# The low part of a second early weight: from VectorE to GpSimd, and its high part earlier on ScalarE

## The chip, the cores and the metric

The kernel runs on one core of a Trainium2 chip. The metric is the device time of one execution in microseconds (us); the time of a kernel is the median of its runs.

## The reference

Two blocks, one behind the other, over 256 tokens of width 1024 in float32. The first has an even and an odd layer (pooling, retention, memory attention, sparse attention). The second has two layers, each of them with this shape:

```python
h = rmsnorm_2(x, norm_mix[i])
proj = h @ w_in[i]                 # na_q, na_k, na_v, latents, gate_a, gate_b
merged = sigmoid(gate_a) * y_a + sigmoid(gate_b) * y_b
x = x + merged @ w_out[i]
x = x + expert_choice_moe(rmsnorm_2(x, norm_moe[i]), ...)
ple_gate = sigmoid(rmsnorm_2(x, norm_ple[i]) @ ple_gate_w[i])
x = x + ple_gate * (p[i] @ ple_w[i])
```

The change lies at the seam between layer 0 and layer 1 of the second block: the last two lines for `i = 0`, and the first two for `i = 1`.

## The kernel before, in words

The five engines run programs of their own, written out by hand, which meet at semaphores. Weights come from HBM through a ring of 12 slots in SBUF (8 KB a partition each), filled in order by SyncE; TensorE counts the units it has begun (`begun`), and SyncE waits for that count before it fills a slot again.

**Split weights.** A projection is computed from a high and a low part of both operands, with three products (high by high, high by low, low by high). A split weight of 1024 x 256 takes two slots. It lands in the first; ScalarE copies it, rounded, into the second (`split` in its program, L1762: the high part), and then VectorE subtracts the high part from the slot of the first, in place (L2160: the low part). GpSimd has a `split` of its own (L2644), with the same subtraction, used for the weights in `HEADS`: gate weights 0 and 3. VectorE's low parts count up the semaphore `lo_ready`, GpSimd's `heads_low`. Where a unit of TensorE is `late`, it waits for the high part alone before its first products and for the low part (`U.low`) in `tile_rest`.

**The seam.** The tokens are two tiles of 128. In `embed_gates`, TensorE multiplies tile 0 and then tile 1 by the four gate weights (`pg` 0 to 3, 256 columns each; L1335 with the high parts of the weights, L1344 with the low parts). Two weights fill a PSUM bank of 512 columns, so there are four evacuations, called gate 0 and gate 1 (tile 0), gate 2 and gate 3 (tile 1). For each, ScalarE makes a tanh (L1878), and VectorE two scalar_tensor_tensor instructions (L2248, which adds 1 and multiplies by the embedding, both operands in SBUF; L2250, which adds the product to x, both in SBUF too). With gate 1 done, tile 0 of x is final: ScalarE sums its squares (L1748), GpSimd makes the root (L2611, L2612), ScalarE scales the rows (L1752), and TensorE transposes them (L956). These transposes stand in TensorE's queue ahead of the last gate product. The transposed tile is split into high and low parts in `tile_high` (ScalarE, L1791) and `tile_parts` (VectorE, L2119 and eight L2124, one operand in PSUM). Tile 1 goes the same way behind gate 3, with its sum of squares (L2100) and its scale (L2105) on VectorE.

Layer 1 opens in `values_start`: tile 0 by the first two weights of `w_in` that are used, `("nav", 0)` and `("nav", 1)`, then the transposes of tile 1 and tile 1 by the same two. These two weights are called `EARLY`, since they are split at the end of layer 0:

```python
HEADS = [("pg", 0), ("pg", 3)]
EARLY = [("nav", 0), ("nav", 1)]
```

Before the change, both parts of nav 0 are made behind gate 0, and both parts of nav 1 ahead of gate 3, behind `tile_high` on ScalarE and `tile_parts` on VectorE. `split_at` numbers the splits that VectorE counts in `lo_ready`. Behind the seam ScalarE issues the small loads of the next layer (behind gate 3), and GpSimd makes eight bias tiles of the neighbourhood attention when they have landed (L2713); VectorE adds the first in L2446.

Of the kernel before, what the change touches and what calls it, by code (L numbers as in the profile page):

```python
# [23 lines left out]
ALU = mybir.AluOpType  # L24
# [26 lines left out]
LAYERS = 2  # L51
# [242 lines left out]
SPLIT_FIRST = [u for u in FIRST_UNITS if u[0] in SPLIT]  # L294

HEADS = [("pg", 0), ("pg", 3)]
EARLY = [("nav", 0), ("nav", 1)]
SPLIT_LAYER = [u for u in LAYER_UNITS + PLE_UNITS if u[0] in SPLIT and u not in HEADS]
# [102 lines left out]
def build(nc, a, out, at):  # L401

    ctx = ExitStack()
    with ctx:
        def sem(name):
            return ctx.enter_context(nc.semaphore(name))
# [177 lines left out]
        rpb_out, biastile_out = sem("rpb_out"), sem("biastile_out")  # L584
        side_in = sem("side_in")
        lo_ready = sem("weights_low")
        heads_low = sem("heads_low")
        uTh_ready = sem("uT_high")
        spare_in = [sem(f"spare_in{i}") for i in range(SPARES)]
        units_in = [sem(f"unit_in{s}") for s in range(RING)]  # L590
# [71 lines left out]
        def slot_at(l, unit, second=False):  # L662

            if l is None:
                n = FIRST_AT[unit] + second
                return n % RING, n // RING + 1, n - RING + 2 if n >= RING else None
            n = FIRST_SLOTS + LAYER_AT[unit] + second + l * PER_LAYER
            return n % RING, n // RING + 1, n - RING + 2

        def split_at(l, unit):  # L670
            return SPLIT_FIRST.index(unit) if l is None else \
                len(SPLIT_FIRST) + SPLIT_LAYER.index(unit) + l * len(SPLIT_LAYER)

        def words_of(name, *i):

            if name == "out":
                return 2 * D
            i = i[0]
            return KC * {"o_gl": 3 * NH, "lat": LATC}.get(name, 256)

        def rows_of_unit(unit):
            return OUT_ROWS[unit[1]][unit[2]][1] if unit[0] == "out" else P
# [13 lines left out]
        def slot_words(s, n, words=ring):  # L696
            return words[:, s * SLOT:s * SLOT + n]
# [23 lines left out]
        def layer_gains(l):  # L721
            return gT[:, GC_L + l * GL:GC_L + (l + 1) * GL]
# [167 lines left out]
        def _(pe):  # L890
# [3 lines left out]
            class Unit:  # L894
# [3 lines left out]
                def __init__(s, l=None, split=None, double=False, late=False):  # L898
                    s.slot, rnd, _ = w.next()
                    s.low = None  # L900
                    if double:
                        pe.wait_ge(units_in[s.slot], 16 * rnd)
                        pe.sem_inc(units_in[w.next()[0]], 16)
                    elif split:
                        if split in HEADS:
                            s.low = (heads_low, HEADS.index(split) + 1 + l * len(HEADS))
                        else:
                            s.low = (lo_ready, split_at(l, split) + 1)
                        s.high, rnd, _ = w.next()
                        if late:  # L910
                            pe.wait_ge(units_in[s.high], 16 * rnd)
                        else:
                            pe.wait_ge(*s.low)
                    else:
                        pe.wait_ge(units_in[s.slot], 16 * rnd)
                    s.first, s.step = True, Unit.before
                    Unit.before = 2 if split or double else 1
# [34 lines left out]
            unit = [None]  # L952
# [779 lines left out]
        def _(act):  # L1732
# [21 lines left out]
            def split(l, *unit):  # L1754

                s0, rnd, _ = slot_at(l, unit)
                s1, _, free = slot_at(l, unit, True)
                act.wait_ge(units_in[s0], 16 * rnd)
                if free is not None:
                    act.wait_ge(begun, free)  # L1760
                n, r = words_of(*unit), rows_of_unit(unit)
                A(slot_words(s1, n, ring_r)[0:r], slot_words(s0, n)[0:r], ACT.Copy).then_inc(units_in[s1], 16)  # L1762
# [24 lines left out]
            def tile_high(l, j, t, gains):  # L1787

                act.wait_ge(uT_psum, 4 * normT_at(l, j) + 2 * t + 2)
                for k in range(4, KC):  # L1790
                    A(uTh_r[:, k, t * P:(t + 1) * P], banks[5 + 2 * t][:, (k - 4) * P:(k - 3) * P], ACT.Copy,  # L1791
                      scale=gains[:, k:k + 1]).then_inc(uTh_ready, 1)
# [209 lines left out]
            for l in range(LAYERS):  # L2002
# [75 lines left out]
                evacuate(l, "pg", 0)  # L2078
                if l + 1 < LAYERS:
                    split(l + 1, *EARLY[0])  # L2080
                evacuate(l, "pg", 1)
                act.wait_ge(x_ple, TT + 4 * l + 2)
                tile_ss(0, x[:, 0, :])
# [2 lines left out]
                evacuate(l, "pg", 2)  # L2086
                if l + 1 < LAYERS:
                    tile_high(l + 1, 0, 0, layer_gains(l + 1))
                    split(l + 1, *EARLY[1])
                evacuate(l, "pg", 3)  # L2090


# [1 line left out]
        def _(dve):  # L2094
# [59 lines left out]
            def split(l, *unit):  # L2154

                s0, _, _ = slot_at(l, unit)
                s1, rnd, _ = slot_at(l, unit, True)
                dve.wait_ge(units_in[s1], 16 * rnd)
                n, r = words_of(*unit), rows_of_unit(unit)
                V.tensor_tensor(slot_words(s0, n, ring_r)[0:r], slot_words(s0, n)[0:r],  # L2160
                                slot_words(s1, n, ring_r).bitcast(F32)[0:r], ALU.subtract).then_inc(lo_ready, 1)
# [111 lines left out]
            for j, plan in enumerate((EVEN_PLAN, ODD_PLAN_V)):  # L2273
                for entry in plan:
# [67 lines left out]
                    elif what == "RT":  # L2342
                        dve.wait_ge(r_tp, h + 1)
                        c, n = RET_CHUNKS[h][0], len(RET_CHUNKS[h])
# [84 lines left out]
            for l in range(LAYERS):  # L2429
                gl = layer_gains(l)  # L2430
                tile_parts(l, 0, 1, gl)
                for entry in LAYER_PLAN:
                    what, h = entry[0], entry[1]
                    i = att_at(l, h) if what in "STV" else None
# [147 lines left out]
                evacuate(l, "pg", 2)  # L2582
                if more:
                    tile_parts(l + 1, 0, 0, layer_gains(l + 1))
                    split(l + 1, *EARLY[1])
                else:
                    dve.wait_ge(lastg_in, 16)
                    store_rows(0)
# [9 lines left out]
        def _(pool):  # L2598
# [36 lines left out]
                steps.link(g.tensor_tensor(ms[:, c], ms[:, c], neghalf[:, 0:1], ALU.pow))  # L2635
                g.tensor_tensor(rstd[:, c], ms[:, c], lrstd[:, c], ALU.mult).then_inc(norm_rstd[t], 1)

            def split(l, name, i):

                s0, _, _ = slot_at(l, (name, i))  # L2640
                s1, rnd, _ = slot_at(l, (name, i), True)
                pool.wait_ge(units_in[s1], 16 * rnd)
                n = words_of(name, i)
                g.tensor_tensor(slot_words(s0, n, ring_r), slot_words(s0, n), slot_words(s1, n, ring_r).bitcast(F32),  # L2644
                                ALU.subtract).then_inc(heads_low, 1)

            def normalise(h, i, buf):
                pool.wait_ge(recip_done, i + 1)
# [3 lines left out]
            for j, plan in enumerate((EVEN, ODD)):  # L2652
                for entry in plan:
# [14 lines left out]
                    elif entry[1:2] == ("e_za",):  # L2668
                        i = entry[2]
# [37 lines left out]
            for l in range(LAYERS):  # L2707
                if l:
                    norm(l, 0)

                pool.wait_ge(side_in, 64 * (l + 1))
                for h in range(NAH):
                    g.tensor_tensor(  # L2713
                        strided(B_at + h * TT * T, P, (T, TT), (GRIDW, 4), (1, GRIDW)),
                        strided(F_at + h * NBIAS + 2 * NADC, P, (-2 * NADC, TT), (NADC, 4), (1, GRIDW)),
                        con("namask").unsqueeze(1).unsqueeze(1).broadcast_to([P, TT, 4, GRIDW]),
                        ALU.add).then_inc(nabias, 1)
                for entry in LAYER:
                    what, h = entry[0], entry[1]
                    if what == "T":  # L2720
                        normalise(h, att_at(l, h), b_S)
                    if what == "T" and h == NAH - 1:
                        pool.wait_ge(lat_ss, l + 1)
                        for n, wd in enumerate((QR, KVR)):
                            stand(pool)
                            steps.link(g.tensor_scalar(lms[:, 2 * n:2 * n + 2], lss[:, 2 * n:2 * n + 2], 1.0 / wd, EPS,
                                                       ALU.mult, ALU.add))
                        g.tensor_tensor(lrstd, lms, neghalf[:, 0:4], ALU.pow).then_inc(lat_rstd, 1)
                norm(l, 1)
                pool.wait_ge(idx_ready, l + 1)  # L2730
                stand(pool)
                with pool.Fori(0, NE // BATCH) as b:
                    for q in range(BATCH):
                        m = l * NE + b * BATCH + q
                        if q == 0:
                            pool.wait_ge(onehot_ready, l * (NE // BATCH) + b + 1)
                        else:
                            pool.wait_ge(comb_psum, m)
                        g.tensor_tensor(prep, onehot[:, :, q, :].unsqueeze(2).broadcast_to([P, TT, 4, CAP]),  # L2739
                                        affh[:, :, bass.ds(b * BATCH + q, 1)].unsqueeze(3)  # L2740
                                        .broadcast_to([P, TT, 4, CAP]), ALU.mult).then_inc(slots_ready, 1)
                split(l, *HEADS[0])
                for t in range(TT):
                    half_root(l, t)
                split(l, *HEADS[1])
            norm(LAYERS, 0)


# [22 lines left out]
```

## Time and profile before

| | |
|---|---|
| time, median of 3 runs | 1879.73 us (1878.81 to 1879.8) |
| the profiled execution | 1878.34 us, span 1876.6 us |
| TensorE busy, mean granted clock | 1547.2 us (82%), 0.941 of full speed |
| VectorE busy | 634.5 us (34%) |
| ScalarE busy | 517.1 us (28%) |
| GpSimd busy | 197.2 us (11%) |
| HBM | 302 GB/s over the span |

The busy times say how much an engine has to do, not whether anything waits for it. The clock is the one that was granted to TensorE, as a share of 2.4 GHz; 0.50 is the lower level, 1.2 GHz. The profile gives each instruction a start and a duration, and in brackets how long its engine had been idle before it and what ended that. An instruction that is held up while it runs shows as a long one, not as an idle engine.

### The profile page before, as it was taken

Reading aid. Unit: us, or ns where it says so; the run is one execution under the profiler, and the core shown is the slowest. Engines: PE = TensorE matmul, PEld = TensorE weight load, DVE = VectorE, ACT = ScalarE, POOL = GpSimd, SP = SyncE. Lnnn points to the kernel's source line nnn. Section 1 sums busy time; section 2 is a strip of 40 time slices with the busy share of each in tenths; the row PEclk is TensorE's granted clock in tenths of the full one; section 3 lists DMA queues with packets and bytes.
Section 4 is the critical chain, followed back from the end, with each engine's and each line's share of the span. In section 5 each row is a group of like instructions: output and inputs, shape, how many; then the busy total and the mean of one; then the engine's idle time right before and its main releaser. Section 6 shows DMA issues by size and latency. Waiting matters only on the chain.

```text
span 1876.6 us, 29888 instructions
## 1 busy us (share of the span) xinstructions
PE 1547.2 (82%) x12670; PEld 1134.7 (60%) x12670; DVE 634.5 (34%) x934; ACT 517.1 (28%) x921; POOL 197.2 (11%) x215
## 2 busy tenths in 40 slices
PE   9999999999999999656665666999998656766667
PEld 8999899998798885222322323998873322323225
DVE  3556654667556452000000002755540000000005
ACT  3433443456444532000000003454521000000003
POOL 1042000011041100000000002411100000000003
PEclk9999999999999999898888989999999897888879
DMA  9364669423555479999999999644499999999994
GB/s 304 125 208 169 203 231 302 130 97 113 181 152 160 136 314 387 427 425 424 425 427 424 428 425 368 192 145 156 179 381 407 424 426 424 427 426 426 427 425 161
DMA packets 166895, 563.67 MB, mean 300 GB/s; under 512 B 10559, under 2 KB 120027, under 8 KB 133896
## 3 DMA queue, kind: packets, MB, share of 16 engines
q1 hardware_dynamic: 161092, 553.88, 76.4%
q10 hardware_dynamic: 5700, 8.31, 1.3%
q8 instruction: 78, 1.28, 0.3%
q14 instruction: 25, 0.20, 0.0%
HBM read 561.08 MB, written 5.23 MB: 302 GB/s over the span
## 4 chain that ended last, share of the span: by engine, by line
PE 57%; DMA 37%; DVE 2%; issue 2%; ACT 1%; POOL 1%; ACTq 0%; POOLq 0%; DVEq 0%; SPq 0%
DMA ring<-in_moe_w 37%; PE bank L1004 25%; PE bank L1272 7%; PE bank L1689 5%; PE bank L956 4%; PE bank L1335 2%; PE bank L1712 2%; PE bank L1119 1%; PE bank L1111 1%; PE bank L1149 1%; PE bank L1544 1%; PE bank L1344 1%; PE bank L1200 1%; PE bank L1084 1%; ACT big L1810 1%
## 5 line engine op out<-in xcount | busy, mean ns | idle before, releaser
L1689 PE MATMUL bank<-ring,big 128*32 128x256 f32 x3840 | 289.0, 452 | 194.0 <-DMA ring<-in_moe_w 192.0
L1004 PE MATMUL bank<-big_r,ring_r 128*128 128x256 f32 (+1 forms) x2856 | 355.4, 284 | 0.0
L1689 PEld LDWEIGHTS bank<-ring,big 128*32 128x32 f32 x3840 | 149.6, 125 | 337.4 <-issue 298.0
L1004 PEld LDWEIGHTS bank<-big_r,ring_r 128*128 128x128 f32 (+1 forms) x2856 | 346.2, 191 | 3.0 <-issue 2.2
L2160 DVE TENSOR_TENSOR ring_r<-ring,ring_r 128x2048 fp32r<-128x2048 f32 (+2 forms) x113 | 261.1, 2316 | 131.3 <-ACT ring_r L1762 129.7
L1810 ACT ACTIVATE big<-bank 128x512 f32<-128x512 f32 (+2 forms) x186 | 87.8, 491 | 546.4 <-PE bank L956 345.8
L1762 ACT ACTIVATE ring_r<-ring 128x2048 fp32r<-128x2048 f32 (+2 forms) x117 | 219.4, 1884 | 15.2 <-issue 7.7
L1712 PE MATMUL bank<-ring,big 128*32 128x512 f32 x1024 | 136.7, 633 | 70.2 <-DMA ring<-in_moe_w 53.4
L2556 DVE SCALAR_TENSOR_TENSOR big<-big,bank 128x256 f32<-128x256 f32 x32 | 13.5, 421 | 465.2 <-ACT big L2063 465.2
L1272 PE MATMUL bank<-ring_r,big_r 128*128 128x512 f32 x576 | 136.6, 396 | 0.7 <-DVE big_r L2167 0.7
L1272 PEld LDWEIGHTS bank<-ring_r,big_r 128*128 128x128 f32 x576 | 107.9, 189 | 25.6 <-DVE ring_r L2160 1.1
L956 PE MATMUL bank<-big 128*128 128x128 f32 (+6 forms) x636 | 102.0, 285 | 24.1 <-ACT big L1810 18.3
L1712 PEld LDWEIGHTS bank<-ring,big 128*32 128x32 f32 x1024 | 26.5, 112 | 157.0 <-DMA ring<-in_moe_w 111.4
L956 PEld LDWEIGHTS bank<-big 128*128 128x128 f32 (+6 forms) x636 | 70.9, 142 | 66.1 <-issue 25.8
L2559 DVE TENSOR_TENSOR big<-big,bank 128x256 f32<-128x256 f32 x32 | 19.2, 600 | 261.5 <-PE bank L1689 261.5
L2739 POOL TENSOR_TENSOR big<-big 128x256 f32<-128x256 f32 x32 | 19.7, 615 | 806.9 <-PE bank L956 599.5
L2063 ACT ACTIVATE big<-bank 128x256 f32<-128x256 f32 x32 | 12.3, 383 | 317.4 <-PE bank L1689 317.4
L1004 PE MATMUL bank<-ring_r,big_r 128*128 128x256 f32 (+1 forms) x816 | 99.2, 281 | 0.0
L1718 PE MATMUL bank<-big 64*128 64x512 f32 x256 | 79.1, 746 | 23.7 <-ACT big L1810 23.7
L1004 PEld LDWEIGHTS bank<-ring_r,big_r 128*128 128x128 f32 x816 | 96.4, 191 | 1.8 <-issue 1.7
L2649 POOL TENSOR_TENSOR big<-big 128x512 f32<-128x512 f32 x40 | 42.4, 1061 | 335.6 <-DVE big L2263 335.6
L1718 PEld LDWEIGHTS bank<-big 64*128 64x128 f32 x256 | 25.9, 217 | 75.0 <-ACT big L1810 55.2
(213 smaller groups left out, 1472.9 us busy)
## 6 DMA issues: line engine op xcount, KB each, us to landing
ring<-in_moe_w SPq DMA_DIRECT2D x120, 2048.0 KB, 23.7
ring<-in_moe_w SPq DMA_DIRECT2D x128, 1024.0 KB, 24.8
ring<-in_w_in SPq DMA_DIRECT2D x28, 1024.0 KB, 5.4
ring<-in_od_w_in SPq DMA_DIRECT2D x22, 1024.0 KB, 5.8
ring<-in_ev_w_in SPq DMA_DIRECT2D x20, 1024.0 KB, 5.7
big<-in_moe_w SPq DMA_DIRECT2D x8, 2048.0 KB, 11.1
ring<-in_ev_w_out SPq DMA_DIRECT2D x8, 1024.0 KB, 4.9
ring<-in_od_cmp_w SPq DMA_DIRECT2D x8, 1024.0 KB, 8.3
```

Of the source, the lines that this page charges most:

```text
L956: return nc.tensor.transpose(dst, src, ident[0:rows, 0:rows])
L1004: ins = unit[0].mark(mm(dst, lhsT, rhs, start=start and n == 0, stop=stop and n == len(terms) - 1))
L1272: ins = U.mark(mm(banks[OUT_BANK[j] + 2 * t + half][:, :], g, wv[:, kk, half * 512:(half + 1) * 512], start=i == 0 and kk == 0 and term == ...
L1335: ins = U.mark(mm(dst, x_[:, k, toks], hi[:, k, :], start=fresh and k == 0 and x_ is uTh_r, stop=False, skip_group_check=True))
L1689: ins = mm(banks[5 + up][32 * j:32 * j + 32, 0:256], xg[:, k, q, :], wv[:, r, 256 * j:256 * (j + 1)], start=k == 0, stop=k == KC - 1)
L1712: ins = U.mark(mm(banks[4][c:c + 32, :], hT[:, r * P + 32 * j:r * P + 32 * j + 32], wv[:, r, half * 512:(half + 1) * 512], start=j == 0, s ...
L1718: mm(banks[2 * t + half][:, :], comb[64 * half:64 * half + 64, t * P:(t + 1) * P], ob[64 * half:64 * half + 64, :], start=False, stop=True ...
L1762: A(slot_words(s1, n, ring_r)[0:r], slot_words(s0, n)[0:r], ACT.Copy).then_inc(units_in[s1], 16)
L1810: return A(dst, src, ACT.Copy).then_inc(s, 1)
L2160: V.tensor_tensor(slot_words(s0, n, ring_r)[0:r], slot_words(s0, n)[0:r], slot_words(s1, n, ring_r).bitcast(F32)[0:r], ALU.subtract).then_ ...
L2649: g.tensor_tensor(buf[:, h % 2], buf[:, h % 2], rsum[:, h % 2, :].unsqueeze(2).broadcast_to([P, TT, T]), ALU.mult).then_inc(probs_ready, 1)
L2739: g.tensor_tensor(prep, onehot[:, :, q, :].unsqueeze(2).broadcast_to([P, TT, 4, CAP]), affh[:, :, bass.ds(b * BATCH + q, 1)].unsqueeze(3) ...
```

## The change

In layer 0 only (`l + 1 < LAYERS`), for nav 1 of layer 1: ScalarE makes the high part behind the one of nav 0, ahead of gate 1, and no longer behind `tile_high`; GpSimd makes the low part behind its split of gate weight 3 and counts it in a semaphore of its own, `early_low`; VectorE makes it no longer. TensorE waits for `early_low` for this unit, and `split_at` leaves it out of VectorE's count. Layer 0's own nav 1 stays as it was. No transfer is added, removed or moved in its queue.

```diff
-        heads_low = sem("heads_low")
+        heads_low, early_low = sem("heads_low"), sem("early_low")
...
         def split_at(l, unit):
-            return SPLIT_FIRST.index(unit) if l is None else \
-                len(SPLIT_FIRST) + SPLIT_LAYER.index(unit) + l * len(SPLIT_LAYER)
+            if l is None:
+                return SPLIT_FIRST.index(unit)
+            n = SPLIT_LAYER.index(unit)
+            return len(SPLIT_FIRST) + n + l * len(SPLIT_LAYER) - (l if n > SPLIT_LAYER.index(EARLY[1]) else max(l - 1, 0))
...
                             s.low = (heads_low, HEADS.index(split) + 1 + l * len(HEADS))
+                        elif l and split == EARLY[1]:
+                            s.low = (early_low, l)
                         else:
...
@@ scalar @@
                 evacuate(l, "pg", 0)
                 if l + 1 < LAYERS:
                     split(l + 1, *EARLY[0])
+                    split(l + 1, *EARLY[1])
                 evacuate(l, "pg", 1)
...
                 if l + 1 < LAYERS:
                     tile_high(l + 1, 0, 0, layer_gains(l + 1))
-                    split(l + 1, *EARLY[1])
                 evacuate(l, "pg", 3)
...
@@ vector @@
                 evacuate(l, "pg", 2)
                 if more:
                     tile_parts(l + 1, 0, 0, layer_gains(l + 1))
-                    split(l + 1, *EARLY[1])
                 else:
...
@@ gpsimd @@
-            def split(l, name, i):
+            def split(l, name, i, low):
...
                 g.tensor_tensor(slot_words(s0, n, ring_r), slot_words(s0, n), slot_words(s1, n, ring_r).bitcast(F32),
-                                ALU.subtract).then_inc(heads_low, 1)
+                                ALU.subtract).then_inc(low, 1)
...
-                split(l, *HEADS[0])
+                split(l, *HEADS[0], heads_low)
                 for t in range(TT):
                     half_root(l, t)
-                split(l, *HEADS[1])
+                split(l, *HEADS[1], heads_low)
+                if l + 1 < LAYERS:
+                    split(l + 1, *EARLY[1], early_low)
```

## Rows read from the trace of the kernel before

**Rows 1.** The page: the chain that ended last, shares of the span by engine.

```profile
PE 57%; DMA 37%; DVE 2%; issue 2%; ACT 1%; POOL 1%; ACTq 0%; POOLq 0%; DVEq 0%; SPq 0%
```

**Rows 2.** That chain in order of time, at the seam: start us, us, what.

```profile
1189.77 2.05 issue
1191.82 0.69 DVE big L2248
```

**Rows 3.** Timeline of VectorE: start us, us, instructions [idle before <- what ended it].

```profile
1171.62 2.16 DVE L2124 SCALAR_TENSOR_TENSOR big_r<-bank,big,big_r 128x128 fp32r<-128x128 f32 x8
1173.82 3.00 DVE L2248 SCALAR_TENSOR_TENSOR big<-big 128x512 f32<-128x512 f32 x1
1176.85 0.69 DVE L2250 SCALAR_TENSOR_TENSOR big<-big 128x512 f32<-128x512 f32 x1
1177.58 2.29 DVE L2160 TENSOR_TENSOR ring_r<-ring,ring_r 128x2048 fp32r<-128x2048 f32 x1
1179.89 0.69 DVE L2248 SCALAR_TENSOR_TENSOR big<-big 128x512 f32<-128x512 f32 x1
...
1187.42 2.16 DVE L2124 SCALAR_TENSOR_TENSOR big_r<-bank,big,big_r 128x128 fp32r<-128x128 f32 x8
1189.61 2.29 DVE L2160 TENSOR_TENSOR ring_r<-ring,ring_r 128x2048 fp32r<-128x2048 f32 x1
1191.82 0.69 DVE L2248 SCALAR_TENSOR_TENSOR big<-big 128x512 f32<-128x512 f32 x1
```

**Rows 4.** Timeline of ScalarE.

```profile
1172.13 1.94 ACT L1762 ACTIVATE ring_r<-ring 128x2048 fp32r<-128x2048 f32 x1
1179.17 0.69 ACT L1878 ACTIVATE big<-bank,big 128x512 f32<-128x512 f32 x1 [5.11 <-PE bank L1344]
1181.34 1.06 ACT L1748 ACTIVATE big<-big 128x1024 f32<-128x1024 f32 x1 [1.49 <-DVE big L2250]
...
1183.42 1.15 ACT L1752 ACTIVATE big<-big 128x1024 f32<-128x1024 f32 x1 [0.93 <-POOL big L2612]
...
1188.67 0.69 ACT L1878 ACTIVATE big<-bank,big 128x512 f32<-128x512 f32 x1
```

**Rows 5.** Timeline of GpSimd.

```profile
1171.63 4.63 POOL L2644 TENSOR_TENSOR ring_r<-ring,ring_r 128x2048 fp32r<-128x2048 f32 x1
...
1198.41 17.51 POOL L2713 TENSOR_TENSOR big<-big 128x512 f32<-128x512 f32 x8 [3.00 <-DMA big<-in_p]
```

**Rows 6.** Timeline of TensorE.

```profile
1184.73 1.03 PE L956 MATMUL bank<-big 128*128 128x128 f32 x8
...
1193.27 1.12 PE L1344 MATMUL bank<-ring_r,big_r 128*128 128x256 f32 x8
1196.25 1.09 PE L956 MATMUL bank<-big 128*128 128x128 f32 x8 [1.86 <-DVE big L2105]
```

**Rows 7.** Busy time by stretch: PE, PEld, DVE, ACT, POOL; granted clock, DMA share, GB/s.

```profile
1172.00:1174.00 2.00, 2.00 (x19) 2.00 (x18) 1.97 (x8) 2.00 (x2) 2.00 (x1) 1.00 0.02 8
1190.00:1200.00 10.00, 7.41 (x60) 6.96 (x59) 8.17 (x16) 3.78 (x6) 2.33 (x4) 1.00 0.82 250
875.20:878.20 3.00, 3.00 (x32) 1.30 (x24) 0.00 (x0) 0.00 (x0) 0.00 (x0) 0.51 0.96 404
```

**Rows 8.** Timelines of GpSimd and VectorE behind the seam, single instructions.

```profile
1200.72 3.24 POOL L2713 TENSOR_TENSOR big<-big 128x512 f32<-128x512 f32 x1
...
1202.83 3.28 DVE L2160 TENSOR_TENSOR ring_r<-ring,ring_r 128x2048 fp32r<-128x2048 f32 x1
```

**Rows 9.** Timeline of TensorE in layer 0's expert loop.

```profile
870.01 2.42 PE L1689 MATMUL bank<-ring,big 128*32 128x256 f32 x32 [3.89 <-DMA ring<-in_moe_w]
874.75 3.58 PE L1689 MATMUL bank<-ring,big 128*32 128x256 f32 x32 [2.32 <-DMA ring<-in_moe_w]
879.64 1.93 PE L1689 MATMUL bank<-ring,big 128*32 128x256 f32 x32 [1.31 <-DMA ring<-in_moe_w]
```

**Rows 10.** Timeline of VectorE, the first use of a bias tile.

```profile
1222.66 0.69 DVE L2446 SCALAR_TENSOR_TENSOR big<-bank,big 128x512 f32<-128x512 f32 x1 [2.64 <-PE bank L1164]
```

## The prediction

> **What bounds the kernel now.** I read the shares of the chain that ended last first: TensorE and the expert-weight DMA carry 94% of it between them [rows 1]. The edit touches one place, the seam between the two layers at 1,160 to 1,200 us, so the question is which engine the chain runs through there. The chain in order of time answers it: it crosses VectorE at 1191.82 us, in the last gate's evacuation (L2248), after 2.05 us marked as issue, in which VectorE was running the split that the change takes away [rows 2, 3]. Then I read each engine's timeline at the seam. VectorE has hardly a hole from 1171.62 to 1180 us and is late again from 1187 us; ScalarE has a hole of 5.11 us before 1179.17 us; GpSimd has nothing between the end of its second split (1176.26 us) and the small norm operations behind ScalarE's sum of squares; TensorE runs without a hole until 1194.39 us and then idles 1.86 us, until the last rows of x are evacuated, normalised and scaled [rows 3 to 6]. So the seam is a chain in which VectorE, ScalarE and TensorE alternate, each almost without slack.
>
> **The change, part by part.** (a) *ScalarE's high part of nav 1* moves from behind tile_high (1186.82 us) to behind the split of nav 0. It costs one copy like that at 1172.13 us, 1.94 us, so about 1174.05 to 1175.95 us, inside the 5.11 us hole [rows 4]. Its weight must have landed: between 1172 and 1174 us the DMA engines are 2% busy, so the early loads are all in [rows 7]. Cost 0. The old copy's removal gives nothing either: the tanh of gate 3 starts at 1188.67 us on TensorE's last product, hardly later than the copy's end. If the cover were gone, the tanh of gate 1 would be late by up to 1.9 us.
>
> (b) *VectorE's low part of nav 1* (2.29 us at 1189.61) is removed. tile_parts ends at 1187.42 + 2.16 = 1189.58 us and the tanh of gate 3 at 1188.67 + 0.69 = 1189.36 us, so L2248 could start at 1189.61 instead of 1191.82: 2.21 us less on this chain [rows 3, 4]. But the transposes behind it (PE L956 at 1196.25) follow TensorE's own products, which end at 1194.39 us. So TensorE gives back 1.86 us at most [rows 6]. Taken alone: -1.9 us.
>
> (c) *GpSimd's low part of nav 1* is added behind its split of gate weight 3. The trace has the same operation on the same shape: 4.63 us at 1171.63 [rows 5]. GpSimd itself has the time: its next work waits for ScalarE's sum of squares, 1181.34 + 1.06 us. TensorE wants the low part only at 1193.27 us [rows 4, 6]. So far 0. What counts is what VectorE does meanwhile. The first L2248 starts at 1173.82 us under the earlier GpSimd split and takes 3.00 us, where its sisters take 0.69. It ends at 1176.82 us, 0.56 us after GpSimd's end (1176.26 us). The eight L2124 under the same split, which take one input from PSUM, keep their usual 2.16 us [rows 3, 5]. So a VectorE operation with both inputs in SBUF stands still until a running GpSimd tensor_tensor is over.
>
> The Trainium skill, page SBUF — State Buffer, section Who interferes with whom, says this as a rule: a VectorE instruction with two SBUF inputs and a GpSimd instruction that reads SBUF exclude each other for the whole instruction, and whichever issues first goes first. By that rule and by these rows the change brings a second such stretch. A reader of the busy shares alone (VectorE 34%, GpSimd 11%) would get -1.9 us here.
>
> Who goes next, when both have work, is in the rows behind the seam. A GpSimd instruction is issued at 1200.72 us, under a split of VectorE's, and ends at 1203.96. VectorE's next split is issued at 1202.83, straight behind that first one, and ends at 1206.11, which is 2.15 us (a whole split of 2.29, less 0.14) after GpSimd's end [rows 3, 8]. So GpSimd, which was waiting, went before VectorE's next: they take turns, one instruction each. So at 1176.26 us the waiting L2248 runs until 1176.82 us; the new split, issued at about 1176.3, then holds until 1176.8 + 4.6 - 0.1 = 1181.3 us; and L2250, issued at 1176.85 us, ends at 1181.3 + 0.56 = 1181.8 instead of 1177.54 us. VectorE is late by 4.25 us [rows 3, 5]. Bounds: if GpSimd kept its turn, 4.6; if VectorE got through without any wait, 0. I take 4.25, by the 3.00 us row.
>
> (d) *Where the delay goes.* Behind L2250 stand the split of nav 0 (1177.58, 2.29) and the evacuation of gate 1 (1179.89), which starts as the split ends (1179.87) and as ScalarE's tanh ends (1179.17 + 0.69 = 1179.86): slack 0. Then ScalarE's sum of squares (1181.34), GpSimd's norm, ScalarE's scale (1183.42 + 1.15 = 1184.57), and TensorE's transposes at 1184.73, which stand in its queue ahead of the last gate product: slack 0.1 [rows 3, 4, 6]. TensorE so gets a hole of about 4.15 us at 1184.7, where it has none. Its queue from there to 1194.39 us shifts to 1198.54; VectorE's own side shifts by 4.15 to 4.25 - 2.21 = about 2.0, to 1198.3 at the transposes. TensorE's side is later: +4.15 - 1.86 = +2.3 us.
>
> (e) *TensorE's clock.* Through the seam it is granted in full (1.00), and the idle of 1.86 us did not change that [rows 7]. A hole of 4.15 us is longer than any that the trace has in its dense stages. The nearest is 3.89 us, in the expert loop: the 32 matmuls that follow it take 2.42 us, the next 32 take 3.58 us, with 0.51 granted (the lower level, 1.2 GHz), and the third 1.93 us again at 2.4 GHz [rows 7, 9]. Price of one such stretch: 3.58 - 1.93 = 1.65 us if all of it lies on busy TensorE, and 0 if it lies in the hole or does not come. The fall can come before the hole ends, so part of it is then free. I take 1.1 us, nearer the upper end.
>
> The Trainium skill, page TensorE: Matmul & The Clock Gate, section Why this matters for your kernels, warns of idle gaps between bursts for this reason. By its rule the fall is to be expected here; the trace agrees for the 3.89 us gap and has no dense stage to show it in.
>
> (f) *Behind the seam.* ScalarE's loads for the next stage are issued behind gate 3 and shift by 4.15 us, so GpSimd's eight bias sums start at about 1202.5 instead of 1198.41 and end some 4 us later than 1215.92; VectorE wants the first at 1222.66 + 2.3 [rows 5, 10]. Hidden. The rest of layer 1 is TensorE's queue until the experts, whose loads wait for it, so a delay passes through whole [rows 1]. The new numbering of the semaphores moves no wait.
>
> Sum: -1.86 + 4.15 + 1.1 = +3.4 us. The profiled execution took 1878.34 us (span 1876.6 and 1.7 around it), 1.4 below the median of the three runs, 1879.73. On the median: 1883.1 us.
>
> **The rivals.**
> - *The change does what it says* (VectorE's turn is not lost, or the new split starts too late to meet anything dear): -1.9 us, 1877.8. For it: the engines' shares. Against: the 3.00 us row, and VectorE has only two-input SBUF work from 1176.85 to 1181.31 us, so wherever the new split falls there it meets some.
> - *Collision, but no fall of the clock*: +2.3 us, 1882.0. For it: no dense stage shows a fall. Against: the gap of 3.89 us.
> - *Clearly slower*: collision, and the low stretch begins when TensorE is already back at work, in the transposes and the last gate product (1189 us on). Then its whole 1.65 us is paid: +3.95, 1883.7; with a second one in a row, 1885.3. It decides from a clock price of about 1.5 us on. For it: after the 3.89 us hole the fall came well inside the work. Against: the hole is long enough to hide the start.
>
> **How the numbers follow.** Collision with part of a low stretch: 0.40, 1883.1. Collision with a whole one or more: 0.26, 1883.7 to 1885.3. Collision alone: 0.21. The change as told: 0.10. Anything else: 0.03. A measurement of this kernel can tell about 0.2%, 3.8 us, from no change, so the boundary lies at 1883.5 us, just above the likeliest. All of the whole-stretch case but a little (0.23), and a fifth of the likeliest (0.07), lie beyond it: slower 0.30. Faster by as much needs twice what the edit can give: 0.02. Range 1881.3 to 1884.6: from the collision alone, less the runs' scatter, to a whole low stretch and the same scatter; it leaves out the change as told and the double stretch. The case of the opposite sign holds little, so the likeliest one's own range is 1882.3 to 1884.0.
>
> **What would show it.** Right: a VectorE L2250 of about 5 us at 1176.9; the split of nav 0 at 1181.8; a hole of TensorE of about 4 us before its transposes at 1188.9; L2248 of gate 3 straight behind tile_parts; no hole of 1.86 us later; perhaps 0.5 granted between 1188 and 1193 us. Wrong: L2250 at 0.69 us, or GpSimd's split stretched instead; or the transposes at 1184.7 as before.

## The result, and the profile after

| | median | runs |
|---|---|---|
| before | 1879.95 us (1878.24 to 1882.68) | 20 |
| after | 1882.20 us (1878.88 to 1886.28) | 20 |

The ratio is 1.0013, with a 95% interval of 1.0007 to 1.0019: 1.3 to 3.6 us slower, which is clear of noise and inside the 0.2% that was called no change. (The ratio is not the quotient of the two medians, here and below.) The medians are 2.25 us apart. The profiled execution of after took 1882.46 us, with a span of 1880.7 us.

In after.py the line numbers are higher: L2164 is the old L2160, L2252 and L2254 the old L2248 and L2250, L1752 and L1756 ScalarE's old sum of squares and scale (L1748 and L1752), L960 the old L956, L1339, L1348 and L1008 the old L1335, L1344 and L1004, and L2647 GpSimd's old split L2644. The experiments that add lines shift them by a few more. The seam begins 0.34 us earlier in this profile than in that of before (L2128 at 1171.28 us against L2124 at 1171.62), so a time of after is read with 0.34 us added.

The chain that ended last, at the seam, in order of time (start us, us, what):

```profile
1176.52 5.00 DVE big L2254
...
1181.71 2.05 issue
1183.76 0.70 DVE big L2252
...
1184.48 0.70 DVE big L2254
...
1185.20 1.16 ACT big L1752 x2
...
1187.28 1.16 ACT big L1756
...
1188.48 1.97 PE bank L960 x8
1190.45 2.45 PE bank L1339 x16
```

VectorE's L2254 is on the chain with 5.00 us, where [rows 3] have 0.69 for the same instruction. The 2.05 us of "issue" has moved: it is now VectorE's split of nav 0, no longer that of nav 1 [rows 2]. GpSimd's timeline shows what held L2254:

```profile
1175.89 5.08 POOL L2647 TENSOR_TENSOR ring_r<-ring,ring_r 128x2048 fp32r<-128x2048 f32 x1
```

This is the new split. It was issued at once behind the earlier one, waited for the L2252 that was ahead of it, and ended at 1180.97 us; L2254 ended 0.55 us later, at 1181.52. TensorE's timeline, answering to [rows 6]:

```profile
1183.50 1.12 PE L1348 MATMUL bank<-ring_r,big_r 128*128 128x256 f32 x8
1188.48 1.97 PE L960 MATMUL bank<-big 128*128 128x128 f32 x8 [3.86 <-ACT big L1756]
1190.10 2.80 PE L1339 MATMUL bank<-ring_r,big_r 128*128 128x256 f32 x16
...
1198.49 1.13 PE L1348 MATMUL bank<-ring_r,big_r 128*128 128x256 f32 x8
1199.46 1.03 PE L960 MATMUL bank<-big 128*128 128x128 f32 x8
...
1207.20 4.96 PE L1008 MATMUL bank<-big_r,ring_r 128*128 128x256 f32 x40
```

A hole of 3.86 us has come at 1184.6 us, and the one of 1.86 us ahead of the second transposes has gone. The first transposes behind the hole take 1.97 us against 1.03, and the products after them 2.80 against 2.15 in the old timeline. The busy times by stretch say why (columns as in [rows 7]; the column after the busy times is the granted clock):

```profile
1184.00:1188.00 4.00, 0.62 (x6) 0.42 (x4) 1.14 (x2) 1.87 (x3) 0.73 (x2) 1.00 0.71 241
1188.00:1191.50 3.50, 3.02 (x14) 3.02 (x15) 2.30 (x4) 2.01 (x6) 0.00 (x0) 0.52 0.00 0
1191.50:1200.00 8.50, 8.50 (x73) 8.50 (x72) 5.31 (x13) 2.62 (x3) 0.74 (x2) 1.00 0.95 317
```

The clock is at its lower level, 1.2 GHz, from about 1188.1 to 1191.5 us.

To compare the seam between kernels I use one distance, called **the seam** below: from the start of VectorE's eight L2124 (L2128 in after) of the gates' second tile to TensorE's first product of layer 1 behind nav (L1004; L1008 in after). Before: 1204.06 - 1171.62 = 32.44 us. After: 1207.20 - 1171.28 = 35.92 us, which is 3.48 more. The sum in the prediction was 3.4; how far that agreement is luck is told under (e) below.

### The profile page after: what moved, and what is told of

Its sections match the earlier page's. It is cut to its first block, busy times and chain, and to the rows that moved or that the text cites. A ratio compares the mean times of both kernels' runs of the same rounds, so it can differ in the third digit from the quotient of the medians.

```text
span 1880.7 us, 29888 instructions
## 1 busy us (share of the span) xinstructions
PE 1549.5 (82%) x12670; PEld 1135.9 (60%) x12670; DVE 636.9 (34%) x933; ACT 517.4 (28%) x921; POOL 202.2 (11%) x216
## 4 chain that ended last, share of the span: by engine, by line
PE 57%; DMA 38%; DVE 2%; issue 1%; ACT 1%; POOL 1%; ACTq 0%; POOLq 0%; DVEq 0%; SPq 0%
DMA ring<-in_moe_w 37%; PE bank L1008 25%; PE bank L1276 7%; PE bank L1693 4%; PE bank L960 4%; PE bank L1716 2%; PE bank L1339 2%; PE bank L1123 1%; PE bank L1115 1%; PE bank L1153 1%; PE bank L1548 1%; PE bank L1204 1%; PE bank L1088 1%; ACT big L1814 1%; PE bank L1348 1%
## 5 line engine op out<-in xcount | busy, mean ns | idle before, releaser
L1693 PE MATMUL bank<-ring,big 128*32 128x256 f32 x3840 | 280.7, 443 | 186.7 <-DMA ring<-in_moe_w 185.4
L1008 PE MATMUL bank<-big_r,ring_r 128*128 128x256 f32 (+1 forms) x2856 | 355.4, 284 | 0.0
L1008 PEld LDWEIGHTS bank<-big_r,ring_r 128*128 128x128 f32 (+1 forms) x2856 | 346.3, 191 | 3.0 <-issue 2.2
L2164 DVE TENSOR_TENSOR ring_r<-ring,ring_r 128x2048 fp32r<-128x2048 f32 (+2 forms) x112 | 259.1, 2319 | 130.7 <-ACT ring_r L1766 129.2
L960 PE MATMUL bank<-big 128*128 128x128 f32 (+6 forms) x636 | 101.1, 284 | 24.7 <-ACT big L1814 18.3
L960 PEld LDWEIGHTS bank<-big 128*128 128x128 f32 (+6 forms) x636 | 71.0, 142 | 65.1 <-DVE big L2563 25.1
L1722 PE MATMUL bank<-big 64*128 64x512 f32 x256 | 88.5, 825 | 23.8 <-ACT big L1814 23.8
L1008 PE MATMUL bank<-ring_r,big_r 128*128 128x256 f32 (+1 forms) x816 | 99.2, 281 | 0.0
L1008 PEld LDWEIGHTS bank<-ring_r,big_r 128*128 128x128 f32 x816 | 96.4, 191 | 1.8 <-issue 1.7
```

Source lines behind the costliest of these rows:

```text
L960: return nc.tensor.transpose(dst, src, ident[0:rows, 0:rows])
L1008: ins = unit[0].mark(mm(dst, lhsT, rhs, start=start and n == 0, stop=stop and n == len(terms) - 1))
L1693: ins = mm(banks[5 + up][32 * j:32 * j + 32, 0:256], xg[:, k, q, :], wv[:, r, 256 * j:256 * (j + 1)], start=k == 0, stop=k == KC - 1)
L1722: mm(banks[2 * t + half][:, :], comb[64 * half:64 * half + 64, t * P:(t + 1) * P], ob[64 * half:64 * half + 64, :], start=False, stop=True ...
```

## The experiments

Times are medians, and the ratio is to the runs of the kernel before on the same chip (median 1879.57 us for 1 to 3 and the first time of 4; 1880.56 for 5, for the 14 matmuls of 6 and for the changed kernel once more in 8; 1880.04 for the second time of 4, for the 8 matmuls of 6 and for 7).

**1. The high part alone** (on the kernel before; VectorE keeps the low part).

```diff
                     split(l + 1, *EARLY[0])
+                    split(l + 1, *EARLY[1])          # scalar
                 evacuate(l, "pg", 1)
...
                     tile_high(l + 1, 0, 0, layer_gains(l + 1))
-                    split(l + 1, *EARLY[1])
```

> The kernel before with one part of the change: ScalarE's high part of nav 1 behind that of nav 0; the low part stays with VectorE ahead of gate 3. Theory A (the cost is the collision of GpSimd's new split with VectorE): the copy lies in ScalarE's hole of 5.11 us, so 0.0 us against before, 0.3 either way. Theory B (the early copy itself makes gate 1 late): at least +1 us, with the tanh of gate 1 behind the copy.

Measured: 1879.09 us, ratio 1.0000 (0.9991 to 1.0009). The interval is 1.7 us wide to either side, so the time alone does not exclude the 1 us of theory B. The profile does: VectorE's first instruction of gate 1 starts 1178.09 - 1169.92 = 8.17 us behind the start of the seam, against 1179.89 - 1171.62 = 8.27 before.

```profile
1178.09 0.69 DVE L2248 SCALAR_TENSOR_TENSOR big<-big 128x512 f32<-128x512 f32 x1
```

So the copy on ScalarE delays nothing, and theory B falls. The profile showed something else, in TensorE's timeline and in the busy times by stretch:

```profile
1194.45 1.87 PE L956 MATMUL bank<-big 128*128 128x128 f32 x8 [1.91 <-DVE big L2105]
1196.63 2.78 PE L1335 MATMUL bank<-ring_r,big_r 128*128 128x256 f32 x16 [0.31 <-DVE big_r L2124]
```

```profile
1194.50:1198.00 3.50, 3.19 (x14) 2.79 (x15) 2.29 (x7) 1.64 (x5) 1.28 (x2) 0.52 0.37 77
```

This kernel has the old hole of 1.9 us, and here a stretch at the low clock (a low stretch, below) follows it: seam 1203.10 - 1169.92 = 33.18 us, 0.74 more than in the profile of before.

**2. No split on GpSimd** (on the changed kernel).

```diff
                     split(l + 1, *EARLY[1])
+                    s0 = slot_at(l + 1, EARLY[1])[0]          # scalar
+                    A(slot_words(s0, 2048, ring_r), slot_words(s0, 2048), ACT.Copy).then_inc(early_low, 1)
...
-                if l + 1 < LAYERS:                             # gpsimd
-                    split(l + 1, *EARLY[1], early_low)
```

> The changed kernel with GpSimd's new split left out: ScalarE copies the first slot of nav 1 in place, rounded, instead (1.9 us more in its hole, no VectorE, no GpSimd). The subtraction of the high part of nav 1 is left out of the computation. Theory A: L2254 at 0.7 us instead of 4.99, no hole of TensorE at 1184 us, and -1.9 us against before, as the edit would give without a collision (1878.0 us). Theory B: still slower than before by 2 us.

Measured: 1877.27 us, ratio 0.9984 (0.9975 to 0.9993). L2256 is this kernel's L2250, L960 the transposes; VectorE and TensorE:

```profile
1177.34 0.69 DVE L2256 SCALAR_TENSOR_TENSOR big<-big 128x512 f32<-128x512 f32 x1
...
1185.28 1.03 PE L960 MATMUL bank<-big 128*128 128x128 f32 x8
```

The 5 us and the hole are gone. Seam 1202.53 - 1172.10 = 30.43 us, 2.01 less than before. This kernel leaves out the subtraction, whose place in time ScalarE's second copy takes, off the chain. Everything that the change costs comes with GpSimd's split.

**3. VectorE's split in its own hole** (on kernel 1).

```diff
                 evacuate(l, "pg", 1)                  # vector
+                if more:
+                    split(l + 1, *EARLY[1])
                 evacuate(l, "pg", 2)
                 if more:
                     tile_parts(l + 1, 0, 0, layer_gains(l + 1))
-                    split(l + 1, *EARLY[1])
```

> High part early on ScalarE, low part on VectorE right behind gate 1, in its hole of 3.9 us, nothing new on GpSimd. The lock works the other way too: GpSimd's first norm instruction at 1182.6 us has to wait for the end of the split at 1183.6, so the norm is 0.85 us late and TensorE's transposes by 0.75. Theory A: -1.86 + 0.75 = -1.1 us against before. If GpSimd's small instructions do not wait: -1.9. Theory B: slower than before.

Measured: 1877.90 us, ratio 0.9990 (0.9981 to 0.9999). VectorE, GpSimd and TensorE:

```profile
1180.55 2.29 DVE L2160 TENSOR_TENSOR ring_r<-ring,ring_r 128x2048 fp32r<-128x2048 f32 x1
...
1181.79 1.10 POOL L2612 TENSOR_SCALAR big<-big 128x1 f32<-128x1 f32 x1 [6.20 <-ACT big L1748]
...
1184.75 1.10 PE L956 MATMUL bank<-big 128*128 128x128 f32 x8 [1.26 <-ACT big L1752]
```

GpSimd's instruction on one column takes 1.10 us instead of 0.19, until 1182.89 us, when the split (1180.55 + 2.29 = 1182.84) is over. The lock works both ways. Seam 31.13 us, 1.31 less than before, for 1.1 in the sum.

**4. The same behind the norm of tile 0** (the rest of the edit as in 3).

```diff
                 evacuate(l, "pg", 1)                  # vector
+                if more:
+                    dve.wait_ge(norm_rstd[0], norm_at(l + 1, 0) + 1)
+                    split(l + 1, *EARLY[1])
```

> As the one before it, but the split on VectorE waits for the norm of tile 0, so it starts at 1183.4 and ends at 1185.7 us, 0.45 us into the evacuation of gate 2. Theory A: norm instructions at 0.19 and 0.54 us, tile_parts 0.45 us late, TensorE's queue still what the second transposes follow: -1.7 us against before, 0.6 better than with the split unguarded. If the lock on GpSimd's small instructions is free, it is 0.2 worse than unguarded instead.

> The version with VectorE's split behind the norm of tile 0, once more, for a narrower interval: -2.2 us against before by the first time it ran, -1.7 by the sum.

Measured: 1876.79 us, ratio 0.9988 (0.9979 to 0.9997), and the second time 1876.88 us, 0.9984 (0.9975 to 0.9993). GpSimd, VectorE and TensorE of the second:

```profile
1181.02 0.19 POOL L2613 TENSOR_SCALAR big<-big 128x1 f32<-128x1 f32 x1 [6.37 <-ACT big L1748]
...
1181.92 2.29 DVE L2160 TENSOR_TENSOR ring_r<-ring,ring_r 128x2048 fp32r<-128x2048 f32 x1 [2.17 <-POOL big L2614]
1184.13 0.69 DVE L2248 SCALAR_TENSOR_TENSOR big<-big 128x512 f32<-128x512 f32 x1
...
1192.93 1.09 PE L956 MATMUL bank<-big 128*128 128x128 f32 x8
```

The split starts as the norm is done, and no idle stands before TensorE's second transposes. Seam 1200.74 - 1169.98 = 30.76 us, 1.68 less than before, for which the sum had -1.7. In the first run of it the low stretch from the experts ended late (1164.75 us) and left TensorE behind at the entrance; its seam was 31.14. Both times this version was faster than the kernel before, and its interval lies wholly below that of the changed kernel (1.0007 to 1.0019); the gap between 3 and 4 is within their intervals.

**5. GpSimd's split behind the norm of tile 0** (on the changed kernel).

```diff
                 if l:                                  # gpsimd
-                    norm(l, 0)
+                    tile_norm(l, 0, 0)
+                    split(l, *EARLY[1], early_low)
+                    tile_norm(l, 0, 1)
...
                 split(l, *HEADS[1], heads_low)
-                if l + 1 < LAYERS:
-                    split(l + 1, *EARLY[1], early_low)
```

> The changed kernel with GpSimd's split of nav 1 moved behind the norm of tile 0, so it runs from about 1183.4 to 1188.0 us. Theory A: gate 1 is free of it (L2254 0.7 us, transposes at 1184.7 as before), but the evacuation of gate 2 (ready at 1185.2) stands still until 1187.9, so tile_parts is 2.7 us late; TensorE waits some 2 us for it, and gate 3 starts 0.4 us later than before: +0.3 us against before, 2 us better than the changed kernel. If the delay came from GpSimd's split being late for TensorE, it would be no better than the changed kernel.

Measured: 1878.97 us, ratio 0.9995 (0.9986 to 1.0004). VectorE and TensorE:

```profile
1184.91 3.28 DVE L2252 SCALAR_TENSOR_TENSOR big<-big 128x512 f32<-128x512 f32 x1 [3.94 <-ACT big L1882]
...
1190.17 3.11 PE L1339 MATMUL bank<-ring_r,big_r 128*128 128x256 f32 x16 [1.89 <-DVE big_r L2128]
```

The collision has moved to gate 2, as expected: 3.28 us against 0.69, and a hole of 1.89 us for TensorE, behind which a low stretch begins (3.11 us for products that take 2.08):

```profile
1191.00:1194.25 3.25, 3.25 (x18) 3.25 (x17) 3.15 (x7) 0.00 (x0) 0.00 (x0) 0.50 1.10 309
```

Seam 1205.24 - 1171.20 = 34.04 us, low stretch and all, which is 1.88 less than in the first profile of after. The delay so comes from where GpSimd's split stands, not from TensorE getting the low part late. The same split on the same engine holds VectorE up for 4.3 us (4.99 against 0.69) in one place and 2.6 in another.

**6. TensorE's hole filled** (on the changed kernel), with 14 and then with 8 matmuls.

```diff
                 if l + 1 < LAYERS:                     # tensor
+                    for _ in range(8):                 # 14 in the first
+                        mm(banks[3][:, 0:T], ident, con("ones"), start=True, stop=True)
                     rows_T(l + 1, 0, 0)
```

> The changed kernel with 14 matmuls without use (identity by ones, 256 columns, into a free bank) ahead of the transposes, in TensorE's hole of 3.9 us; 14 by 0.22 us is 3.1, so they delay nothing. They keep the granted clock at 1.00. If the clock's fall costs 1.1 to 1.6 us where it comes: 1.1 to 1.6 us faster than the changed kernel, +2.1 to +2.3 on before less that, and less scatter between runs. If the fall is rare or free: the same time as the changed kernel.

Measured with 14: 1882.77 us, ratio 1.0013 (1.0004 to 1.0022). The expectation took one matmul for half as long as it is: the 14 took 6.21 us (28 records, two for each) and put the transposes at 1189.54 us, 1.3 us behind the rows' end. The clock stayed at 1.00; what that saved, the overshoot took: seam 1206.79 - 1171.09 = 35.70 us. The time alone says nothing here.

```profile
1183.49 6.21 PE L1409 MATMUL bank<-big 128*128 128x256 f32 x28
1189.54 1.04 PE L960 MATMUL bank<-big 128*128 128x128 f32 x8
```

> The changed kernel with 8 matmuls without use in TensorE's hole in place of 14. A float32 matmul of 256 columns turned out to be two passes, 0.43 us in all, so 14 took 6.05 us and made the transposes 1.2 us late; 8 take 3.5 and end ahead of the rows. Expected: granted clock 1.00 from the hole to the next layer, transposes to first L1008 in 17.25 us as with 14, transposes at the same place as in the changed kernel, and 1.2 to 1.5 us faster than the changed kernel: +1 to +2.1 against before. If the fall of the clock costs nothing on the median, the same as the changed kernel, +2.3 to +2.5.

Measured with 8: 1880.94 us, ratio 1.0006 (0.9997 to 1.0015). TensorE, and its busy time by stretch:

```profile
1183.23 3.62 PE L1409 MATMUL bank<-big 128*128 128x256 f32 x16
1188.03 1.10 PE L960 MATMUL bank<-big 128*128 128x128 f32 x8 [1.18 <-ACT big L1758]
1188.88 2.15 PE L1339 MATMUL bank<-ring_r,big_r 128*128 128x256 f32 x16
...
1205.35 3.88 PE L1008 MATMUL bank<-big_r,ring_r 128*128 128x256 f32 x31
```

```profile
1187.00:1191.50 4.50, 3.47 (x30) 3.47 (x31) 2.75 (x6) 2.69 (x6) 0.00 (x0) 1.00 0.21 38
```

The clock stays in full, and the seam is 1205.35 - 1170.84 = 34.51 us: 2.07 more than before, and 1.41 less than in the first profile of after. This splits the loss into the collision, 2.07 us, and the clock, 1.41 us in that profile. The split rests on the profiles: the interval of this kernel's times overlaps that of after, so the times do not show the clock's part.

**7. GpSimd's split in two halves** (on the changed kernel).

```diff
+                if low is early_low:                   # gpsimd
+                    for c in (slice(0, n // 2), slice(n // 2, n)):
+                        ins = g.tensor_tensor(slot_words(s0, n, ring_r)[:, c], slot_words(s0, n)[:, c],
+                                              slot_words(s1, n, ring_r)[:, c].bitcast(F32), ALU.subtract)
+                    ins.then_inc(low, 1)
+                    return
```

> The changed kernel with GpSimd's new split as two instructions of 1024 columns, 2.3 us each. If the engines take turns: L2254 waits for the first half (about 2.85 us instead of 4.99), the second half goes next, and VectorE's split of nav 0 waits for it (about 4.4 us instead of 2.29), so the delay stays 4.25 us and the time that of the changed kernel, +2.3 to +2.9. If VectorE, once served, kept its turn: only 2.2 us of delay, and about 0 against before.

Measured: 1883.15 us, ratio 1.0020 (1.0010 to 1.0029). GpSimd and VectorE:

```profile
1175.16 2.88 POOL L2649 TENSOR_TENSOR ring_r<-ring,ring_r 128x1024 fp32r<-128x1024 f32 x1
...
1175.81 2.78 DVE L2254 SCALAR_TENSOR_TENSOR big<-big 128x512 f32<-128x512 f32 x1
...
1178.00 2.84 POOL L2649 TENSOR_TENSOR ring_r<-ring,ring_r 128x1024 fp32r<-128x1024 f32 x1
...
1178.62 4.37 DVE L2164 TENSOR_TENSOR ring_r<-ring,ring_r 128x2048 fp32r<-128x2048 f32 x1
```

L2254 at 2.78 and the split at 4.37 us, for 2.85 and 4.4 expected: each engine goes once, then the other. Cutting the operation spreads the delay and hardly shortens it: gate 1 begins 1182.91 - 1170.55 = 12.36 us behind the start of the seam, against 12.48 in after.

**8. Both kernels once more.**

> The changed kernel once more, as the yardstick on this chip and for a second profile: +2.3 us against before if no low stretch of the clock falls on the seam, +3.4 to +4.0 where one does. L2254 at 5.0 us in both.

> The changed kernel a third time, for its seam: L2254 at 5.0 us and a hole of 3.9 to 4.7 us again; low clock behind the hole, as in both profiles so far, if a hole of this length always brings it; 17.25 us from the transposes to the first L1008 if not.

> The kernel before once more, for a second profile of its seam: 17.5 us from the transposes of tile 0 to the first L1004 without its 1.86 us idle, if no low stretch of the clock falls behind that idle; up to 1.6 us more if one does, as in the kernel with the high part early, where it came at 1194.5 us.

Measured: after 1883.03 us, ratio 1.0013 (1.0004 to 1.0022), and a third profile, of a run of 1884.42 us; before, a second profile, of a run of 1878.65 us. TensorE in the third profile of after:

```profile
1188.79 1.97 PE L960 MATMUL bank<-big 128*128 128x128 f32 x8 [4.64 <-ACT big L1756]
1190.41 3.76 PE L1339 MATMUL bank<-ring_r,big_r 128*128 128x256 f32 x16
```

TensorE in the second profile of before, and one stretch of it:

```profile
1193.86 1.09 PE L956 MATMUL bank<-big 128*128 128x128 f32 x8 [1.90 <-DVE big L2105]
1195.69 3.62 PE L1335 MATMUL bank<-ring_r,big_r 128*128 128x256 f32 x16 [0.73 <-DVE big_r L2124]
```

```profile
1196.00:1199.25 3.25, 3.25 (x17) 3.25 (x17) 3.22 (x7) 1.93 (x2) 3.22 (x3) 0.50 0.00 0
```

The seams of all profiles side by side:

| kernel | seam us | low clock at the seam |
|---|---|---|
| before, two profiles | 32.44, 33.69 | none; behind the 1.9 us hole |
| high part alone | 33.18 | behind the 1.9 us hole |
| after, three profiles | 35.92, 37.10, 37.19 | behind the new hole, in each |
| two halves | 35.91 | behind the new hole |
| after, hole filled with 14; with 8 | 35.70; 34.51 | none |
| GpSimd's split behind the norm | 34.04 | behind its 1.9 us hole |
| no split on GpSimd | 30.43 | none |
| VectorE's hole; behind the norm, twice | 31.13; 31.14, 30.76 | none |

Outside the seam the profiles do not follow the edits: the seam starts between 1169.34 us (before, second profile) and 1172.10 us (no split on GpSimd), and from its end to the end of the span it is 672.2 to 674.2 us in all fourteen.

## Why the prediction was right, point by point

**(a), (b), the copy and the removed split.** Shown. The copy alone gives a ratio of 1.0000, and the edit without its collision gives -2.01 us at the seam, against -1.86 taken and 2.21 as VectorE's own side. The prediction took TensorE's last product to end at 1194.39 us, from the row's start and length, which is 0.16 us late: without the hole the transposes come 0.96 us behind the start of that product (1194.79 against 1193.83 in 2), not 1.12.

**(c), the collision.** Shown, in place and in size: L2254 (L2250 in the prediction) ended at 1181.52 us, 1181.86 on the scale of before, for 1181.8 forecast, and in all three profiles it took 5.0 us. Taking GpSimd's split away removes it, moving the split moves it (5), and halving shows the turns (7). The Trainium skill, page SBUF — State Buffer, section Who interferes with whom, has this lock as a rule; the trace agrees, in both directions (4.99 to 5.00 us for 0.69, and 1.10 us for 0.19 on GpSimd).

**(d), where the delay goes.** Shown. The first transposes were 4.09 us late (1188.48 + 0.34 against 1184.73), for 4.15 forecast. Through the queue that leaves +2.07 us with the clock held up, for +2.3 forecast; of the 0.2, 0.16 is the same closeness of the products.

**(e), the clock.** The fall came in each of the four profiles that have the open hole, with 0.50 granted behind it, and in neither of the two with the hole filled. The term of 1.1 us was mis-sized twice, and the two errors partly cancel.

First, the price of the fall is not 1.1 us but 1.4, 2.6 and 2.7 in the three profiles of after (seam less 34.51). In the first the low clock lasted 3.4 us, in the two others nearly 7. The second profile of after:

```profile
1186.00:1192.75 6.75, 5.62 (x27) 5.62 (x28) 4.24 (x11) 2.80 (x6) 0.00 (x0) 0.50 0.33 87
```

In these two TensorE stood ready earlier and its hole was longer, 4.66 and 4.64 us, while the transposes start 17.2 us behind the start of the seam in all three. The length of the hole does not settle it: with two halves it was 4.47 us, and the low clock lasted 3.4 us, at a price of 1.4. The stretch of the expert loop that gave the price already held more than the prediction read in it [rows 9]:

```profile
870.00:871.25 1.25, 1.24 (x24) 0.95 (x28) 0.00 (x0) 0.00 (x0) 0.00 (x0) 1.00 1.01 433
871.50:878.00 6.50, 4.18 (x43) 1.63 (x35) 0.42 (x1) 0.38 (x1) 0.00 (x0) 0.50 0.99 418
```

The clock was down from 871.4 us on, so the first 32 matmuls lost 2.42 - 1.93 = 0.49 us beside the 1.65, and 2.32 us of the low stretch lay in an idle of TensorE, where it costs nothing.

Second, the step held that the idle of 1.86 us does not change the clock, from one profile. It does in others: two further profiles with that hole show a low stretch behind it, in seams that are 0.74 and 1.25 us longer. So the change trades a hole that sometimes brings a fall for one that brought it each time. On the mean of three profiles each, the falls cost 2.2 us after and 0.7 before, a difference of 1.6 for the 1.1 of the sum. That the first two profiles give 3.48 for 3.4 is therefore partly luck: the one of before has no fall, and the one of after has the cheapest. The falls of the old hole may also be why the versions without either hole gained more than -1.1, -1.7 and -1.9 us in their medians; that is argued from the seams, not tested.

**What stays open.** The mean seam of after is 36.7 us (three profiles) and of before 33.1 (three with the old hole), 3.6 us apart, and the timed runs give 1.3 to 3.6 us. The profiles are few. The 20 runs of after scatter more than those of before (standard deviation 2.03 against 0.99 us), as a term that depends on the moment of the fall would make them. The repeats leave that open: 1.55 us for after and 1.25 for before on the same chip, 1.19 with 14 matmuls in the hole, and on another chip 1.33 with 8 matmuls and 1.16 for before. What decides whether a hole of 1.9 us brings a fall, and whether the low clock lasts 3.4 or nearly 7 us, no run here shows.

**(f), behind the seam.** GpSimd's bias tiles began at 1203.25 us, which is 1203.59 on the scale of before, for 1202.5 forecast. No wait for them showed. VectorE's first use still waits for TensorE, and is 1225.80 + 0.34 - 1222.66 = 3.48 us late, which is the whole difference of the seams:

```profile
1225.80 0.69 DVE L2450 SCALAR_TENSOR_TENSOR big<-bank,big 128x512 f32<-128x512 f32 x1 [2.64 <-PE bank L1168]
```

**The rivals.** The change as told (-1.9) was what the kernel without the collision did. Collision without a fall (+2.3, 1882.0 us) did not occur in a profile, except with the hole filled. But the measured median, 1882.20 us, lies nearer to that rival's number than to the 1883.1 of the likeliest case, so the time alone does not choose between the two: the profiles do. The whole low stretch (+3.95) was nearer to two of the three profiles of after (+4.66 and +4.75 on the first of before) than the part of one.

## What to carry to other kernels

An engine's share of busy time does not say whether work can be moved to it: look in the trace for an instruction that is longer than its sisters while the other engine runs, since that one row (3.00 us against 0.69), with the length of GpSimd's split and the order of the turns, priced the collision to 0.1 us. Between VectorE and GpSimd, place a long operation in a stretch where the other engine waits, or where VectorE takes one of its inputs from PSUM (the eight L2124 kept their 2.16 us under GpSimd's split), and mind the small operations on the chain too: 0.9 us was lost on a norm of one column. A hole in TensorE's stream can cost more than its length: where the clock fell behind one, it was 0.7 to 2.7 us more in these profiles. And one profile does not show what a kernel does: the old hole passed without a fall in the first profile and brought one in the next.

## What the runs showed of the hardware

- When VectorE has instructions with two SBUF inputs queued and GpSimd has a tensor_tensor, the two alternate, instruction by instruction, and the one that waits goes before the next of the other, even where that next one was ready (2.78 and 4.37 us in two halves; 5.00 us in one piece).
- TensorE's clock fell to 1.2 GHz in a dense stage behind a hole of only 1.91 us (high part alone, from 1194.6 us) or 1.89 us (GpSimd's split behind the norm, from 1191.0 us), and behind one of 1.90 us and a second of 0.73 us (before, second profile, 1195.9 to 1199.3 us); behind 1.86 and 0.73 us in the first profile of before it did not.
- The low level lasted 3.4 us behind holes of 3.86 us and 4.47 us, and nearly 7 us behind holes of 4.64 and 4.66 us, although TensorE worked without a break once the hole was over.
- A float32 matmul of 256 columns is recorded twice and takes 0.44 us in all at 2.4 GHz (14 of them: 28 records, 6.21 us).
